# Gate and up products of a two-layer decoder trunk by Strassen's scheme, in two passes of 516 tokens

## What is computed

```python
def swiglu(h, w_gate_up, w_down):
    gu = h @ w_gate_up
    return (jax.nn.silu(gu[..., :D_FF]) * gu[..., D_FF:]) @ w_down

# every layer: x += mixer(rmsnorm(x)); x += swiglu(rmsnorm(x))
# D_MODEL = 1024, D_FF = 2816, all in float32
```

## Time and profile before

| what | us |
|---|---|
| median of 3 runs (2575.05 to 2576.61) | 2576.51 |
| span of the profiled execution | 2574.6 |
| TensorE busy in it | 2540.4 |
| VectorE busy | 1127.2 |
| GpSimd busy | 1096.8 |
| ScalarE busy | 553.2 |

### The profile page before, as it was taken

One profiled execution on the slowest core, in us unless ns is written; L12 is line 12 of the kernel. 1 busy time (PEld: TensorE's weight loads), 2 busy tenths in 40 slices (PEclk: granted clock), 3 DMA queues, 4 the chain that ended last, 5 costly groups with the idle time before them and its releaser, 6 DMA issues.

```text
span 2574.6 us, 42753 instructions
## 1 busy us (share of the span) xinstructions
PE 2540.4 (99%) x16331; PEld 2337.5 (91%) x16331; DVE 1127.2 (44%) x2266; ACT 553.2 (21%) x1275; POOL 1096.8 (43%) x701
## 2 busy tenths in 40 slices
PE   8999999999999999999999999999999999999999
PEld 6877766666999999999999987999999999999999
DVE  3478556676163333333333350663633333333333
ACT  5211156666130000000000151322200000000001
POOL 4233136555854333444433253436743344433340
PEclk9999999999999999999999999999999999999999
DMA  5223257775302111111111111111111111111111
GB/s 174 68 77 104 82 177 238 217 233 158 91 26 67 46 44 49 49 49 49 41 45 43 33 50 35 56 42 33 52 49 48 49 49 49 41 45 44 49 33 67
DMA packets 218877, 189.86 MB, mean 74 GB/s; under 512 B 29475, under 2 KB 171555, under 8 KB 218500
## 3 DMA queue, kind: packets, MB, share of 16 engines
q1 hardware_dynamic: 200980, 161.86, 21.5%
q10 hardware_dynamic: 17776, 26.38, 2.9%
HBM read 171.19 MB, written 17.01 MB: 73 GB/s over the span
## 4 chain that ended last, share of the span: by engine, by line
PE 73%; DVE 2%; POOL 1%; ACT 1%; issue 0%; ACTq 0%; POOLq 0%; DVEq 0%
PE ps L542 67%; PE ps L587 1%; PE ps L589 1%; PE ps L588 1%; DVE hs L485 1%; PE ps L2118 0%; PE ps L1345 0%; DVE acc_sq L477 0%; PE ps L1375 0%; DVE Xl L515 0%; PE ps L1323 0%; PE ps L2315 0%; DVE VM_EARLY L2248 0%; POOL Wl L398 0%; POOL Xl L515 0%
## 5 line engine op out<-in xcount | busy, mean ns | idle before, releaser
L542 PE MATMUL ps<-Xh,Wh 128*128 128x256 f32 (+2 forms) x2712 | 871.3, 321 | 4.6 <-ACT sg L1843 3.9
L542 PE MATMUL ps<-Xl,Wh 128*128 128x256 f32 (+2 forms) x2712 | 867.3, 320 | 0.0
L542 PE MATMUL ps<-Xh,Wl 128*128 128x256 f32 (+2 forms) x2712 | 866.3, 319 | 0.0
L395 POOL TENSOR_TENSOR Wh<-raw,zeros 128x1024 fp32r<-128x1024 f32 x178 | 353.8, 1987 | 1055.0 <-PE ps L542 780.0
L542 PEld LDWEIGHTS ps<-Xh,Wh 128*128 128x128 f32 x2712 | 510.1, 188 | 7.0 <-ACT sg L1843 4.6
L542 PEld LDWEIGHTS ps<-Xl,Wh 128*128 128x128 f32 x2712 | 510.2, 188 | 0.7
L542 PEld LDWEIGHTS ps<-Xh,Wl 128*128 128x128 f32 x2712 | 510.7, 188 | 0.0
L398 POOL TENSOR_TENSOR Wl<-raw,Wh 128x1024 fp32r<-128x1024 f32 x178 | 440.7, 2476 | 14.0
L1915 DVE TENSOR_TENSOR Hl<-hf,Hh 128x392 fp32r<-128x392 f32 (+1 forms) x132 | 181.6, 1376 | 464.9 <-ACT Hh L1851 464.9
L542 PE MATMUL ps<-Hh,Wh 128*128 128x392 f32 (+2 forms) x1056 | 340.5, 322 | 0.0
L542 PE MATMUL ps<-Hl,Wh 128*128 128x392 f32 (+2 forms) x1056 | 338.1, 320 | 0.0
(11 more groups left out here) (256 smaller groups left out, 2465.6 us busy)
## 6 DMA issues: line engine op xcount, KB each, us to landing
raw<-in_w_gate_up SPq DMA_DIRECT2D x88, 512.0 KB, 3.8
raw<-in_w_down SPq DMA_DIRECT2D x44, 512.0 KB, 3.6
kring_home<-in_cache_a_k SPq DMA_DIRECT2D x64, 256.0 KB, 3.9
ring<-in_cache_a_v SPq DMA_DIRECT2D x64, 256.0 KB, 3.2
raw<-in_w_in_even SPq DMA_DIRECT2D x20, 512.0 KB, 3.9
raw<-in_w_in_c SPq DMA_DIRECT2D x16, 512.0 KB, 3.8
xs<-in_x_prompt SPq DMA_DIRECT2D x8, 512.0 KB, 8.9
out_v_prompt<-zt ACTq DMA_DIRECT2D x16, 256.0 KB, 2.6
```

The source lines that it names most:

```text
L395: pool.tensor_tensor(h[:, :], r[:, :], zeros[:, :].to_broadcast([P, 1024]), ALU.add).then_inc(split_high, 1)
L542: ins = nc.tensor.matmul(out, w, x, start=(j == 0), stop=(j == len(pairs) - 1))
```

## The change

**Products.** Gate and up weights of a step (1024 x 256 each) and 516 tokens are each cut in 2 x 2 blocks: 4 row blocks of 128 by 128 columns of weight, 4 row blocks by 258 tokens of activation. The four results per matrix come from seven block products instead of eight, in the variant with few sums. VectorE forms four weight combinations per matrix and step (`sums`: s1, the overwritten raw half, s2, s4), and, once a pass, four combinations of the activations (`operand_sums`: two scalings of 516 columns and four differences of 258, each waiting for the one before). Each of the seven weight factors is rounded on ScalarE (`high`) and its remainder is taken on VectorE (`low_dve`, products 1, 3, 4, 5) or GpSimd (`low_pool`, products 0, 2, 6) into a ring of nine buffers `Rh`, `Rl` of 512 columns. A product is a chain of 4 x 3 = 12 matmuls of 258 columns. The products are called G0 to G6 (gate) and U0 to U6 (up) below; each kind has five banks (`BANKS`), and G2 and G3 go into the banks of G0 and G1 after ScalarE has copied those out to `held`.

**Combination.** Seven results are added to four on VectorE, seven operations per kind: `pair_sums`, `first_sums`, `second_sums`, `last_sum`. Silu goes from bank to `sg`, and the gating overwrites `sg`.

**Passes.** The loop of 11 steps runs twice a layer, for tokens 516 to 1031 and then for 0 to 515; weights are loaded and split in both. The operands of a pass fill nearly all of `Xh` and `Xl`, so those of the second pass are written after the last product of the first. The 16 down chains of a step come between the gate and the up products of the next step; those of a pass' last step stand behind it.

**Around it.** The projections finish block 2 first, then 1, then 0 (`LAST_BLOCKS`), since the first pass takes the later tokens; operands of the first pass are made behind the last six chains. The preparation of the gMLP stage (`mixing_*`) and the output transposes (`early_pe`, `finish_behind`) have new places: eight output tiles in the first step of layer 1's second pass, ten behind its last down chains.

The core of the diff:

```diff
+HN = 258
+HT = 2 * HN
+HALVES = (HT, 0)
+RING = 9
...
+        def sums(dve, f, kind, h, i):
+            a0, a1 = rawg if kind == "G" else rawu
+            dve.tensor_tensor(s1[:, :], a1[:, 0:512], a1[:, 512:1024], ALU.add).then_inc(f["sums"].sem, 1)
+            f["sums"].wait(dve, done + 1)
+            dve.tensor_tensor(a1[:, 0:512], a0[:, 0:512], a1[:, 0:512], ALU.subtract).then_inc(f["sums"].sem, 1)
+            dve.tensor_tensor(s2[:, :], s1[:, :], a0[:, 0:512], ALU.subtract).then_inc(f["sums"].sem, 1)
+            f["sums"].wait(dve, done + 3)
+            dve.tensor_tensor(s4[:, :], a0[:, 512:1024], s2[:, :], ALU.subtract).then_inc(f["sums"].sem, 1)
...
+        def operand_sums(dve, f, g, h, j):
+            f["x_lo"].wait(dve, 16 * h + (2, 4)[h] * j)
+            for x, m in enumerate((j, j + 4)):
+                dve.scalar_tensor_tensor(hs[:, x, :], xT[:, m, c0:c0 + HT], gains[:, g, m:m + 1], acc_all[:, c0:c0 + HT],
+                                         ALU.mult, ALU.mult).then_inc(f["x_sum"].sem, 1)
...
...
+            def product(kind, h, i, c):
+                if c in (2, 3):
+                    f["copied"].wait(pe, t * 4 + 2 * w + c - 1)
...
+                elif kind == "G" and c > 4:
+                    f["hid"].wait(pe, t * 4 - 4 + c - 2)
...
+                for j in range(4):
+                    nc.tensor.matmul(out, Rh[q][:, cols], xh, start=j == 0, stop=False)
+                    nc.tensor.matmul(out, Rh[q][:, cols], xl, start=False, stop=False)
+                    last = nc.tensor.matmul(out, Rl[q][:, cols], xh, start=False, stop=j == 3)
...
+            def downs(h, i, within):
+                    elif j == 5:
+                        f["comb"].wait(pe, t * 14 + 17)
+                    elif j > 2:
+                        f["silu"].wait(pe, t * 4 + 4 + {3: 1, 4: 2, 6: 3, 7: 4}[j])
...
+                def step(i):
+                    for c in range(7):
+                        product("G", h, i, c)
+                    side(h, i)
+                    if not is_first(i):
+                        downs(h, i - 1, True)
+                    for c in range(7):
+                        product("U", h, i, c)
+                loop_steps(pe, step)
+                downs(h, STEPS - 1, False)
...
+            if h == 0:
+                for j in range(4):
+                    for x in range(4 * j, 4 * j + 4):
+                        add(0, STEPS - 1, x)
+                    operand_sums(dve, f, g, 1, j)
+                    operand_low(dve, f, 1, j, range(4))
+                    for k in ((), (1,), (3, 4), (5,))[j]:
+                        low_dve(dve, f, "G", 1, 0, k)
```

## The result

The changed kernel takes **2729.3 us** (median of 4 runs, 2728.0 to 2732.9), the kernel before 2576.6 beside it. The ratio is 1.059, with a 95% interval of 1.058 to 1.061: slower by 153 us. The forecast was 2650, slower by 74, with a range up to 2725. The direction was right. The size was off by 79 us, and the time lies 4 us outside the range. The profiled execution spans 2726.0 us. All times are medians of each kernel's executions; one of the four of experiment 4 took 3054.6 us at a mean granted clock of 0.74 and is left out of its median.

The account below looks back on a forecast made before the run. The prediction took TensorE's own stream as the bound before the change. From 2574.6 us: minus 122 (stream), plus 104 (half-step waits), 43 (turns), 35 (heads), 8 and 6 (ends, rest) gave 2649, forecast 2650; range 2555 to 2725.

Parts of the forecast that it names:

- The walk through a middle half step: One middle half step followed through every engine's queue: TensorE waits 2.6 us, times 40 half steps, plus 104 us.
- the lock: VectorE operations with two SBUF inputs and GpSimd operations exclude each other, taking turns: four sums end at 9.7, not 6.4 us.
- 258 columns cost 0.118 us: Price of one feed-forward matmul: 264 make a half step of 31.2 us, 44 make 1373 us, minus 122 us on TensorE.
- Clock: ... 3: Longer idling at turns and heads may lower TensorE's clock, one earlier slow stretch may go: 3 us in all.
- Turns: Between the two passes of each layer: 17 us stall plus 4.5 in the first half step, two times 21.5, plus 43 us.
- 8 operations of about 0.6 more: ScalarE's squares (layer 0) or output copies (layer 1) ahead of U5's rounding in a turn's first half step: within 4.5 us more.
- Heads: Start of each layer's feed-forward: TensorE waits 8 us, first half step loses 11.5, 2 cost before; two heads, plus 35 us.
- Outside the feed-forward stages: From layer 0 into the gMLP stage, 8 VectorE remainders meet GpSimd's 2.4 us operations: 3 us; tail 0.
- 1 (TensorE stays the bound): Middle half steps: collisions fall into VectorE's slack, wait between 0 and 0.75 us, period under 32; 0.35 gives 2560 us; chance 0.20.
- 2 (VectorE is the bound): Middle half steps: GpSimd's 10 operations each cost VectorE 1.2 us, period 36, wait 4.8, kernel 2738 us; chance 0.11.
- 3 (the clock gives way in every half step): Short gaps of every step lower TensorE's clock, losing 1.7 us each: wait 4.3, kernel 2718 us; chance 0.10.
- 4 (the weight load sets the price): Weight load sets 0.130 us a matmul of 258 columns, 139 us more: kernel 2789 us; chance 0.03.

Follow-up runs that it names:

- experiment 4: Changed kernel with gate product 0's copy moved earlier and VectorE's four up-weight sums placed behind the gate combinations: 2645.1 us.
- experiment 1: Changed kernel with GpSimd's weight remainders cut from 512 to 64 columns after the first half step: 2651.9 us.
- experiment 2: Changed kernel with ScalarE copying gate product 0 ahead of the first down weight's and fourth hidden block's roundings: 2749.0 us.
- experiment 3: Changed kernel with VectorE's four up-weight sums behind the gate combinations and ScalarE's silus ahead of those sums' roundings: 2685.8 us.
- experiment 5: Kernel of experiment 4 with the copy of gate product 1 also moved ahead of down weight roundings 1 to 3: 2621.9 us.
- Experiment 6: Changed kernel with blocks of 256 tokens instead of 258, 8 tokens left out of the feed-forward stages: 2724.7 us.
- Experiment 9: Kernel of experiment 8 with idle matmuls inside gaps, 55 and 45 at each head, 12 and 30 at each turn: 2610.8 us.
- experiment 11: Kernel of experiment 8 with the second pass' operands made for 16 columns only, the rest left out: 2582.7 us.
- experiment 7: Kernel of experiment 5 with idle matmuls added at heads and turns, 45, 25, 58 at each turn, 55 and 45 at each head: 2637.3 us.
- experiment 8: Kernel of experiment 5 with layer 0's second-pass group of 8 squares spread between ScalarE's roundings and copies: 2616.2 us.

## Why the prediction was right or wrong, point by point

**The walk through a middle half step** was right. From the first gate product's start at 1002.27, worked out as 23 spacings before the last matmul of products 0 and 1 at 1005.03, the four silus start at 10.4, 14.2, 15.0 and 17.4 us; the walk had 10.65, 14.4, 15.2 and 17.6. The sums start at 4.2 (3.8) and end at 9.9 (9.7). The waits are 2.8 us (2.6), the second of them before down chain 7 and released by sg, as the prediction put it. Experiments 1 to 5 confirm its parts one by one: the lock alone 1.8 us of it, the copy the rest. This term was mis-sized by 8 us of 104, about the 0.1 us that the matmul behind each of the two waits loses.

**The step that failed first: "258 columns cost 0.118 us".** I took one price per column, 0.457 ns, from spacings at 384 and 256 columns and scaled it. In the window of the earlier trace rows the kernel before has 0.1181 us in the mean of its spacings at 256 columns, 0.1750 at 384 and 0.1787 at 392: a slope of 0.445 ns a column and 4 ns besides for each matmul, which one price hides where a product is cut into narrower pieces. The 24 spacings of the earlier trace rows gave 0.1175, too few. The line through the widths gives 0.119 at 258; measured is 0.1203. This is 24 us over the 264 x 44 matmuls, the saving being 98 instead of 122. Experiment 6 shows that 256 columns in the very same chains cost 0.118.

**The step that failed second: "Clock: ... 3".** I saw in the earlier trace rows that an idle stretch of 2 us can be followed by a granted clock of 0.66, wrote in four stretches of longer stalls, and gave them 3 us in all. (The kernel before has a second stretch of low clock in layer 0, 10 us long and behind no wait, which my rows don't show; see the last section.) Summed over the starts, slow spacing behind the gaps costs 6.2 and 4.7 us at the heads and 6.6 and 6.0 at the turns: 23.5 (21 if only spacings of up to 0.35 us are counted, as in experiments 9 and 11). Experiment 9 brought most of the clock back at the heads and 4 to 5.5 us with it, so at least a part of the 23.5 is the clock on the path; how much the turns would give back stayed open, since bank 7 was not free in the first of their gaps (experiment 7).

**Turns:** the waits of the turn in layer 1 are 21.5 us where 23.5 were forecast (17 + 4.5 + 2), those in layer 0 28.0. From the end of the last up product at 1140.1 to product 0's last quarter at 1173.3 are 33.1 us, forecast 31.5 with the lock; the gaps ahead of that product are 16.5 us above the spacing, forecast 17. What was missed is the size of "8 operations of about 0.6 more" in layer 0: the squares do not follow each other at 0.4 or 0.6 us but 1.13, each waiting for GpSimd (experiment 8). The wait behind them is 9.3 us; it stands before up product 2 and ends with ScalarE's copy. In layer 1, where there are none, 2.7 us came of the 4.5.

**Heads:** waits of 20.6 and 22.2 us against 19.5. The sum came out, but in good part by luck, since only its first term is where the walk put it: 7.5 us ahead of product 0's last quarter (forecast 8). The walk had the other 11.5 us ahead of U0, U2, U4 and U5. The trace has 5.9 us ahead of gate product 2 in both layers, then 5.5 us ahead of up product 1 and 1.0 ahead of up product 2 in layer 0, and 8.1 us ahead of up product 2 in layer 1. In layer 0:

```profile
765.20 0.55 PE L1965 MATMUL ps<-Xh,Rh 128*128 128x258 f32 x1 [5.72 <-ACT held L2034]
...
782.82 0.55 PE L1965 MATMUL ps<-Xh,Rh 128*128 128x258 f32 x1 [5.35 <-DVE wT L2353]
...
761.37 3.42 ACT L1901 ACTIVATE Xh<-thold 128x258 fp32r<-128x258 f32 x8
```

The copy that frees gate product 0's bank stands behind eight roundings of operands on ScalarE (the third row), which the walk of the head left out. The low clock, 10.9 us in the two heads, was not in this term either.

**Outside the feed-forward stages** I had 3 us and it was 13. The first weights' remainders of the attention's projection now come late (TensorE idles 4.7 us between 640 and 740 us, 0.6 before), and so do the low parts that feed the mixing stage (6.6 in the list of waits) and its projection (5.9). The prediction priced the new orders of these projections at nothing and named no cover for them. The tail gave 8 us back; some 4 of them are the transposes that moved into layer 1's turn. These parts were read from the trace alone, and no experiment took them apart.

**The rivals.** 1 (TensorE stays the bound): no; period 34.54, not under 32. But the moves of experiments 3 to 5 turned the changed kernel into it, at 31.73. 2 (VectorE is the bound): no; with another order of the same work its period is 31.73. 3 (the clock gives way in every half step): no; the windows show 1.00 with gaps of 1.7 and 1.1 us from start to start in every half step. What the Trainium skill, TensorE: Matmul & The Clock Gate, section on psum-queue depth-cycling, describes does not show in these loops. The clock falls in and behind longer gaps, those of heads and turns above all, and, without such a gap, in the preparation of the gMLP stage (last section). 4 (the weight load sets the price): no; 0.1203, not 0.130.

Of the signs named beforehand these came: loop period 34 (34.54), the wait before product 2 by the copy, the wait before chain 7 by sg, sums of 1.66 to 1.77 us beside GpSimd. The gap of 15 to 20 us in the middle of each layer came as three gaps, 16.5 us together, the last two ended by Xl and the longest 7.3; taken alone they are under the 8 us that the prediction named as the sign of being wrong. The forecast's own span ended at 2705, with a fifth either way allowed for heads and turns; they were 43% over. The range went on to 2725 for the sake of rival 3.

## What to carry to other kernels

Seven products for eight saved TensorE a fifteenth of its time here and moved VectorE's load from 44% to 73%, and the loss was set by neither total but by the order of the work on the helpers: walk one loop turn through every queue, and look for what stands ahead of the operation that frees a bank, and for VectorE operations with two inputs in SBUF beside operations of GpSimd. Of two waits of one chain, removing the first alone was worth nothing. Price a narrower matmul at its own width, not by the column, and add to every new stall of some microseconds the slow stretch behind it.

## What the runs showed of the hardware that I had not expected

258 columns cost 0.1203 us where 256 cost 0.1181 in the same chains: 2 columns for 2.2 ns, against 0.445 ns a column between 256 and 384. Why was not taken apart.

A matmul that starts behind a wait, even of 1 us, has its successor 0.22 us later instead of 0.12, at a granted clock of 1.00.

The granted clock in the loops stayed at 1.00 with TensorE busy 8.55 and 9.29 of 10 us, and fell to 0.50 to 0.66 at the heads and turns, where gaps of 6 to 9 us stand between short runs of matmuls.

It also fell where TensorE waited for nothing. From 800.73 us on, the kernel before runs pairs of short matmuls for the gMLP stage, two every 0.42 us and none of them after a wait; from 804.8 on they come at the low clock, and so do the down matmuls of 384 columns behind them, 0.32 us apart instead of 0.175. The changed kernel has the same in layer 0's last half step, behind waits of 1.8 and 2.8 us. First the kernel before, then the changed one:

```profile
800.00:810.00 10.00, 10.00 (x41) 7.44 (x40) 0.99 (x2) 1.19 (x2) 0.65 (x1) 0.74 0.18 52
...
1530.00:1540.00 10.00, 7.90 (x27) 5.50 (x27) 3.57 (x7) 3.20 (x7) 1.34 (x2) 0.70 0.41 150
1540.00:1550.00 10.00, 10.00 (x52) 9.33 (x52) 3.21 (x8) 0.60 (x1) 0.00 (x0) 0.61 0.01 2
```
